# Inner layer norms with features on partitions, and the second half of the merge gate ahead of the key transposes

## What is computed

```python
def layer_norm(x, g, b):
    mu = jnp.mean(xf, axis=-1, keepdims=True)
    var = jnp.mean(jnp.square(xf - mu), axis=-1, keepdims=True)
    y = (xf - mu) * lax.rsqrt(var + LN_EPS) * g + b
...
merged = sigmoid(gate_a + b_gate[0]) * y_a + sigmoid(gate_b + b_gate[1]) * y_b   # token_mixer
return merged @ w_o
...
for l in range(DEPTH):                       # 2 layers
    h = layer_norm(ALPHA * h + mix, ln1_g[l], ln1_b[l])
    f = swiglu(h, ...) if l % 2 == 0 else moe_swiglu(h, ...)
    h = layer_norm(ALPHA * h + f, ln2_g[l], ln2_b[l])
return h[:, N_META:]
```

## Time and profile before

| | |
|---|---|
| median of 3 runs | 2019.66 us (2018.73 to 2020.70) |
| the profiled execution, its own time | 2018.01 us |
| its span, first to last instruction | 2016.3 us |
| TensorE matmul busy | 1914.1 us (95%) |
| VectorE busy | 1400.5 us (69%) |
| ScalarE busy | 1092.7 us (54%) |
| mean granted TensorE clock | 0.963 |
| HBM read | 486.74 MB, 242 GB/s over the span |

### The profile page before, as it was taken

One profiled execution on the slowest core, in us unless ns is written; L12 is line 12 of the kernel. 1 busy time (PEld: TensorE's weight loads), 2 busy tenths in 40 slices (PEclk: granted clock), 3 DMA queues, 4 the chain that ended last, 5 costly groups with the idle time before them and its releaser, 6 DMA issues.

```text
span 2016.3 us, 29184 instructions
## 1 busy us (share of the span) xinstructions
PE 1914.1 (95%) x11315; PEld 1684.1 (84%) x11315; DVE 1400.5 (69%) x1160; ACT 1092.7 (54%) x800; POOL 9.3 (0%) x21
## 2 busy tenths in 40 slices
PE   7899999899989899996999999999999999999995
PEld 6889999799978799996787887878878788787884
DVE  3555465744455456566788888888888788787886
ACT  3534344343434453442676767767767667676773
POOL 0000000000000000000000000000000000000000
PEclk9989999899988899996999999999999999999998
DMA  7535334363647358342798998989989999899992
GB/s 242 174 121 184 131 126 168 105 209 126 203 70 178 105 161 211 126 153 97 285 364 324 358 362 312 367 306 347 366 302 357 327 348 359 297 368 335 325 364 82
DMA packets 219258, 491.20 MB, mean 244 GB/s; under 512 B 7932, under 2 KB 12792, under 8 KB 219176
## 3 DMA queue, kind: packets, MB, share of 16 engines
q1 hardware_dynamic: 216416, 482.44, 69.8%
q0 software_dynamic: 1360, 5.25, 0.8%
q10 hardware_dynamic: 1400, 2.33, 0.5%
HBM read 486.74 MB, written 1.05 MB: 242 GB/s over the span
## 4 chain that ended last, share of the span: by engine, by line
PE 52%; DVE 1%; issue 0%; ACT 0%; DVEq 0%; ACTq 0%
PE ps L568 10%; PE ps L570 10%; PE ps L569 10%; PE ps L839 5%; PE ps L841 5%; PE ps L842 5%; PE ps L829 1%; PE ps L854 1%; PE ps L853 1%; PE ps L873 0%; PE ps L874 0%; PE ps L789 0%; DVE ag_lo L1708 0%; ACT ag_hi L941 0%; PE ps L861 0%
## 5 line engine op out<-in xcount | busy, mean ns | idle before, releaser
L1641 DVE TENSOR_TENSOR w_lo<-raw,w_hi 128x2048 fp32r<-128x2048 f32 x336 | 763.5, 2288 | 146.3 <-ACT w_hi L941 146.2
L941 ACT ACTIVATE w_hi<-raw 128x2048 fp32r<-128x2048 f32 x336 | 639.0, 1918 | 208.7 <-PE ps L570 113.4
L348 DVE TENSOR_TENSOR w_lo<-raw,w_hi 128x2048 fp32r<-128x2048 f32 (+2 forms) x128 | 278.9, 2189 | 209.9 <-ACT w_hi L341 204.4
L568 PE MATMUL ps<-hT_hi,w_lo 128*128 128x272 f32 (+1 forms) x1392 | 406.6, 292 | 10.0 <-DVE w_lo L348 3.2
L570 PE MATMUL ps<-hT_hi,w_hi 128*128 128x272 f32 (+1 forms) x1392 | 403.8, 290 | 0.0
L569 PE MATMUL ps<-hT_lo,w_hi 128*128 128x272 f32 (+1 forms) x1392 | 403.7, 290 | 0.0
L568 PE MATMUL ps<-w_hi,xg_lo 128*128 128x512 f32 x896 | 360.3, 402 | 2.4 <-issue 2.4
L569 PE MATMUL ps<-w_lo,xg_hi 128*128 128x512 f32 x896 | 354.8, 396 | 0.0
L570 PE MATMUL ps<-w_hi,xg_hi 128*128 128x512 f32 x896 | 354.7, 396 | 0.0
L341 ACT ACTIVATE w_hi<-raw 128x2048 fp32r<-128x2048 f32 (+2 forms) x128 | 233.7, 1832 | 191.8 <-PE ps L570 153.6
L568 PEld LDWEIGHTS ps<-hT_hi,w_lo 128*128 128x128 f32 x1392 | 267.5, 192 | 13.2 <-issue 8.0
(11 more groups left out here) (231 smaller groups left out, 1959.4 us busy)
## 6 DMA issues: line engine op xcount, KB each, us to landing
raw<-in_moe_w_gate SPq DMA_DIRECT2D x112, 1024.0 KB, 6.6
raw<-in_moe_w_up SPq DMA_DIRECT2D x112, 1024.0 KB, 6.4
raw<-in_moe_w_down SPq DMA_DIRECT2D x112, 1024.0 KB, 5.9
raw<-in_w_in SPq DMA_DIRECT2D x64, 1024.0 KB, 8.5
raw<-in_ffn_w_gate SPq DMA_DIRECT2D x10, 1024.0 KB, 5.3
raw<-in_ffn_w_up SPq DMA_DIRECT2D x10, 1024.0 KB, 5.1
raw<-in_ffn_w_down SPq DMA_DIRECT2D x10, 1024.0 KB, 5.2
raw<-in_w_pa SPq DMA_DIRECT2D x8, 1024.0 KB, 5.1
```

The lines of the kernel that those rows point to most:

```text
L348: nc.vector.tensor_tensor(w_lo[:, u % HALVES, 0:k * n], raw[:, u % RAW, 0:k * n], w_hi[:, u % HALVES, 0:k * n].bitcast(F32), ALU.subtract) ...
L568: nc.tensor.matmul(dst, l_lo, r_hi, start=start, stop=False)
L941: return nc.scalar.activation(dst, src, ACT.Copy, **kw)
L1641: tt(w_lo[:, at % HALVES, :], raw[:, at % RAW, :], w_hi[:, at % HALVES, :].bitcast(F32), ALU.subtract).then_inc(lo_ready, 1)
```

## The change

1. The residual of the inner norms is kept transposed and in float32 (`hF`, features on partitions). The start puts x through PSUM into hF and from there into hT_hi. h_tok exists for the experts alone.
2. An inner norm (`feature_norm`, `norm_sums`) adds the product to ALPHA * hF straight from PSUM, squares on ScalarE (`squares`), adds feature tiles elementwise and lets TensorE sum over partitions with a matrix of 1/1024, which gives mean and mean square in every partition. The last unit of wo1 and fd1 is computed bank by bank. Variance, reciprocal and root are passes over 272 (256) columns. Centring, scaling, gain and bias and the hi/lo split go by groups of feature tiles (1, 1, 2, 2, 2), and the first matmuls of the next product wait by group.
3. The two units of weights that come next are split inside the norm (`next_weights`).
4. In layer 1 the router reads hF, a new set x_tok transposes hF back to tokens, ScalarE makes x_hi and ALPHA * h_tok from it, VectorE x_lo.
5. The set gta1 moves from behind gr1 to ahead of g_kt, on every engine and in the stream of weights.
6. POOL's queue loads broadcast rows only for the last norm.

```diff
@@ trunk, buffers and stream @@
+        hF = sb(ctx, "hF", [P, KT, T])
+        acc = sb(ctx, "acc", [P, 4, T])
-        h_tok = sb(ctx, "h_tok", [P, 3, D])
...
             add_cols(w_in, COL["gate_a"])
+            add_cols(w_in, COL["gate_a"] + COLS)
             pair(w_in, COL["gr"])
-            add_cols(w_in, COL["gate_a"] + COLS)
...
-                local("gvt1"); local("g_kt"); local("g_sc")
+                local("gvt1"); weights("gta1", 2); local("g_kt"); local("g_sc")
...
-                weights("wo0", 2); weights("wo1", 2); local("wot0"); local("wot1")
-                local("h1t0"); local("h1t1")
+                weights("wo0", 2); weights("wo1", 2); local("wo_ln")
...
-                    local("route"); local("rank")
+                    local("route"); local("x_tok"); local("rank")
...
+        NORM_GROUPS = [(0, 1), (1, 2), (2, 4), (4, 6), (6, 8)]
+        def norm_tmp(norm, a, b):
+            if norm == 1:
+                return (gT_s, aT_f)[a // 4][:, a % 4:a % 4 + b - a, width(0)]
+            return sgA[:, a:b, width(norm // 2)]
@@ tensor: feature_major, by_bank and normed @@
+                    if by_bank and k0 + kn == depth:
+                        for m in range(4):
+                            for k in range(kn):
+                                last = step(k, m)
+                            if m < 3:
+                                last.then_inc(bank_full, 1)
+                    else:
+                        for k in range(kn):
+                            if normed is not None:
+                                pe.wait_ge(norm_lo_ready, NG * normed + norm_group(k0 + k) + 1)
+                            for m in range(n // P):
+                                last = step(k, m)
@@ tensor @@
+            def norm_sums(l, name, norm):
+                pt = begin(l, name)
+                cols, mean = width(l), table("mean")
+                pe.wait_ge(sums_ready, 2 * norm + 1)
+                nc.tensor.matmul(pt[:, 0, cols], mean, acc[:, 0, cols], start=True, stop=False)
+                pe.wait_ge(summed, 5 * norm + 4)
+                nc.tensor.matmul(pt[:, 0, cols], mean, hF[:, 6, cols], start=False, stop=False)
+                pe.wait_ge(summed, 5 * norm + 5)
+                nc.tensor.matmul(pt[:, 0, cols], mean, hF[:, 7, cols], start=False, stop=True).then_inc(mean_full, 1)
...
@@ tensor, main order @@
                 back(l, (("gvt1", "gv1"),), (srT[:, 4:8, :],), 3)
+                feature_major(l, "gta1", hT_hi, hT_lo, cols)
                 key_tokens(l, "g_kt", None, k_tail)
...
-                feature_major(l, "gta1", hT_hi, hT_lo, cols)
                 pe.wait_ge(o_ready, 2 * l + 1)
...
-                feature_major(l, "wo1", m_hi, m_lo, cols, inside=(4, lambda: back(l, (("wot0", "wo0"),), (sgA[:, 0:4, :],), tiles)))
-                back(l, (("wot1", "wo1"),), (sgA[:, 4:8, :],), tiles)
-                transposes(l, ("h1t0", "h1t1"), h_tok, tiles, norm=2 * l)
+                feature_major(l, "wo1", m_hi, m_lo, cols, by_bank=True)
+                norm_sums(l, "wo_ln", 2 * l)
@@ scalar @@
-                    copy(dst[:, 4 * i:4 * i + 4, width(l)], pt[:, :, width(l)]).then_inc(act_done, 1)
+                    copy(hF[:, 4 * i:4 * i + 4, :], pt[:, :, 0:T]).then_inc(act_done, 1)
+                    act.wait_ge(act_done, r + 1)
+                    copy(dst[:, 4 * i:4 * i + 4, :], hF[:, 4 * i:4 * i + 4, :]).then_inc(x_split, 1)
...
+            def squares(l, names, norm, ahead):
+                r, _ = take(l, names[0])
+                act.wait_ge(summed, 5 * norm + 1)
+                nc.scalar.activation(norm_tmp(norm, 0, 4), hF[:, 0:4, cols], ACT.Square).then_inc(squared, 1)
+                signed_off(r)
+                ahead()
+                nc.scalar.activation(idle_sqrt[:, :], idle_sqrt[:, :], ACT.Sqrt)
+                for m in range(4):
+                    act.wait_ge(summed, 5 * norm + 2 + m)
+                    nc.scalar.activation(norm_tmp(norm, 4 + m, 5 + m), hF[:, 4 + m:5 + m, cols], ACT.Square).then_inc(squared, 1)
+                signed_off(number[l, names[1]])
+            def feature_norm(l, name, norm):
+                act.wait_ge(mean_full, norm + 1)
+                nc.scalar.activation(acc[:, 0, cols], bank(number[l, name])[:, 0, cols], ACT.Square).then_inc(mean_squared, 1)
+                act.wait_ge(inverse_ready, norm + 1)
+                nc.scalar.activation(acc[:, 1, cols], acc[:, 1, cols], ACT.Sqrt).then_inc(deviation_ready, 1)
+                for i, (a, b) in enumerate(NORM_GROUPS):
+                    act.wait_ge(scaled_ready, NG * norm + i + 1)
+                    for k in range(a, b):
+                        y = norm_tmp(norm, k, k + 1)[:, 0, :]
+                        if l == 0:
+                            nc.scalar.activation(hT_hi[:, k, cols], y, ACT.Identity, scale=ln_col(norm, 0, k), bias=ln_col(norm, 1, k))
+                        ins = nc.scalar.activation(hF[:, k, cols], y, ACT.Identity, scale=ln_col(norm, 0, k), bias=ln_col(norm, 1, k))
+                    ins.then_inc(norm_ready, 1)
...
+            _, pt = take(1, "x_tok")
+            copy(x_hi[:, :, :].rearrange("p t (b n) -> p (t b) n", b=2), pt[:, :, :]).then_inc(x_hi_ready, 1)
+            copy(h_tok[:, :, :].rearrange("p t (b n) -> p (t b) n", b=2), pt[:, :, :], scale=float(ALPHA)).then_inc(act_done, 1)
@@ vector: feature_norm @@
+                r = number[l, names[1]]
+                pt = bank(r)
+                split.upto(ends[r])
+                for m in range(4):
+                    if m < 3:
+                        dve.wait_ge(bank_full, 3 * norm + m + 1)
+                    else:
+                        full(dve, r)
+                    h = hF[:, 4 + m, cols]
+                    stt(h, h, float(ALPHA), pt[:, m, cols], ALU.mult, add).then_inc(summed, 1)
+                    if m == ahead_at:
+                        ahead()
+                    if m == 1:
+                        dve.wait_ge(summed, 5 * norm + 3)
+                        settle()
+                        step(tt(acc[:, 0, cols], acc[:, 0, cols], hF[:, 4, cols], add))
+                        dve.wait_ge(squared, 5 * norm + 2)
+                        step(tt(acc[:, 1, cols], acc[:, 1, cols], norm_tmp(norm, 4, 5)[:, 0, :], add))
+                        settle()
+                        tt(acc[:, 0, cols], acc[:, 0, cols], hF[:, 5, cols], add).then_inc(sums_ready, 1)
+                dve.wait_ge(squared, 5 * norm + 3)
+                dve.wait_ge(sums_ready, 2 * norm + 1)
+                tt(acc[:, 1, cols], acc[:, 1, cols], norm_tmp(norm, 5, 6)[:, 0, :], add).then_inc(sums_ready, 1)
...
+                if ahead_at is None:
+                    ahead()
...
+                dve.wait_ge(mean_squared, norm + 1)
+                step(stt(acc[:, 1, cols], pt[:, 1, cols], float(LN_EPS), acc[:, 0, cols], add, ALU.subtract))
+                settle()
+                nc.vector.reciprocal(acc[:, 1, cols], acc[:, 1, cols]).then_inc(inverse_ready, 1)
...
+                centre(0)
+                centre(1)
+                dve.wait_ge(deviation_ready, norm + 1)
+                scale(0)
+                scale(1)
+                centre(2)
+                scale(2)
+                low(0)
+                low(1)
+                centre(3)
+                scale(3)
+                low(2)
+                centre(4)
+                scale(4)
+                signed_off(r)
+                low(3)
+                low(4)
...
+                feature_norm(l, ("wo0", "wo1"), "wo_ln", 2 * l, lambda: next_weights("wo1"), 0)
+                    feature_norm(l, ("fd0", "fd1"), "fd_ln", 1, lambda: next_weights("fd1"), None)
+            dve.wait_ge(act_done, number[1, "x_tok"] + 1)
```

More of the change, by code:

```diff
@@ L83, in host_constants @@
         ident=np.eye(P), cos=np.cos(ang), sin=sign * np.sin(ang), xi=xi, xi_squared=xi ** 2, zeta=zeta, mask=mask,
-        restart=np.broadcast_to(restart, (P, T)), before=(p[:, None] < p[None, :]), ones=np.ones((P, P)),
+        restart=np.broadcast_to(restart, (P, T)), before=(p[:, None] < p[None, :]), ones=np.ones((P, P)), mean=np.full((P, P), 1.0 / D),
         iota=np.broadcast_to(np.arange(2 * P), (P, 2 * P)),
@@ L222, in trunk @@
         plan = sb(moe, "plan", [1, 4], I32)
+        h_tok = sb(moe, "h_tok", [P, 2, D])
+        rows = sb(moe, "rows", [P, 2, D])
         moe.close()
@@ L596, in next_unit, with feature_major @@
                 return unit(w_hi, s, k, n), unit(w_lo, s, k, n), k, n
-            def feature_major(l, name, x_hi_, x_lo_, cols, depth=KT, made_by=None, inside=None, bank_free=None):
+            def feature_major(l, name, x_hi_, x_lo_, cols, depth=KT, made_by=None, normed=None, bank_free=None, by_bank=False):
                 if bank_free:
@@ L720, in _ @@
             pe.wait_ge(x_landed, 48)
-            transposes(0, ("ht0", "ht1"), h_tok, 3)
+            transposes(0, ("ht0", "ht1"), x_tok, 3)
             for l in range(DEPTH):
@@ L1804, in _ @@
```

(5 more changed lines are left out.)

282 lines of the change are left out of this document (127 added, 155 removed).

## The result

The changed kernel took **2006.05 us**, the median of 5 runs (1998.03 to 2007.0); the kernel before, on the same chip, 2018.88 us, the median of 5. The ratio of the runs is 0.9926, interval 0.9914 to 0.9938; that is 14.9 us less, where the two medians differ by 12.8. It is faster, the forecast of 2000.7 us is 5.4 us too low, and the range of 1991 to 2009 holds it.

What follows compares the result with a forecast made beforehand. TensorE, busy 95% of the span, bounds the kernel; gate move -7.9, norms -5.6, -5.2, -1.4, start +1.15 sum to -18.95 us from 2018.01, 1999.1; with 1.65 for the median, 2000.7 us, range 1991 to 2009.

Steps and rivals of the forecast that it cites:

- T0: Last matmul of the product ahead of a norm (w_o, ffn_w_down); first gate matmul forecast 12.5 us after it.
- the price of 0.75 us for a sum: Float32 mean matmul in the norms: 0.56 or 0.98 us at two clock levels, 0.75 taken.
- the far end of 2.2: Norms' reciprocal over 272 columns: 1.75 us taken, 2.2 kept as the upper end of its range.
- In the other norms it cost 7 us of VectorE beside matmuls that did not wait: nothing: Removing gain and bias on token rows in norms other than layer 1's w_o norm saves no time.
- the forecast's own signs of being wrong: Chain from T0 above 16 us, low clock after a norm beyond 5.3 us, or experts over 2 us different.
- its 1.15 us: Start: an extra ScalarE copy for each half of x delays the first matmul 1.15 us, or 0 if hidden.
- The forecast's own ends: Spreads for reciprocal, mean matmuls, slow clock after restarts and start; together 1990 to 2008 us.
- The scores follow dense work; I take them at half their present: Gate move: scores fall from 3.64 and 3.72 us to 1.9 and 2.0 us.
- rival 3: Gate move: key wait becomes a w_lo wait and the lower clock comes anyway; 2005.6 us, chance 0.10.
- 1 (all passes cheap): Norms: 272-element passes all alike, reciprocal included, and mean matmuls at full clock; 1994.5 us, chance 0.12.
- 2: ScalarE's functions ping-pong: Square outside Sqrt's table adds table loads in each norm, 7.7 us; 2008.4 us, chance 0.12.
- 4: Slower: hand-overs between engines over some 20 dependent norm steps; 2024.7 us at 0.4 us more each, chance 0.04.

Runs made afterwards that it cites:

- recip_twice: The changed kernel with the wide reciprocal issued a second time in each inner norm, into a row that nothing reads; 2013.81 us.
- norms_only: The changed kernel with gta1 put back behind gr1, so norms and start alone; 11.3 us below the kernel before.
- gate_only: The kernel before with only gta1 moved ahead of the key transposes, nothing of the norms; 8.4 us below its kernel before (2019.04).
- before_warm: The kernel before with 14, 14 and 10 unread float32 matmuls in TensorE's long pause of each norm; ratio 0.9986, 2.8 us.
- early_gate: The changed kernel with ScalarE's and VectorE's split of gta1's first weight unit put ahead of their waits for the decays; 1998.62 us.
- lo_early: early_gate plus VectorE's two w_lo of each inner norm parted, one ahead of the last four banks, one behind the last add; 1988.61 us.
- lo_early_warm: lo_early with matmuls that nothing reads added in TensorE's pauses around the norms; 0.9842 of the kernel before, against 0.9845 for lo_early.
- after_again: The changed kernel itself, unaltered, profiled once more; the profiled execution took 2000.57 us, 5.7 less than the first.

## Why the forecast was right, and where it was not

**The norms: right.** First gate matmul after T0, 12.5 us forecast, 12.6 measured; behind ffn_w_down 12.9 and 12.9. recip_twice shows that the reciprocal is on that chain. The 12.6 holds only where the sums behind w_o fall into the lower clock, as in both executions of the change; in norms_only they did not, and it was 10.9. So the price of 0.75 us for a sum, between the two ends, is in part luck. Reciprocal 1.75 forecast, 1.85 measured, so the far end of 2.2 falls. So does the estimate of 2.3 us from the Trainium skill (VectorE: DVE Perf Modes, "First, the fixed hardware budget"). ScalarE's passes with scale and bias from memory took 0.60 us where I had 0.43 from a row with neither; in layer 0 they lay beside VectorE's work. The Trainium skill (ScalarE: Activation LUTs, "What ACT_TABLE_LOAD costs") has a fixed part for each activation and 93 ns for each operand read from memory, which makes an estimate of 0.60 us; the trace agrees, and for this pass the page was the better source. Sums: they start 0.46 us apart at the full clock and 0.91 at the lower, for 0.56 and 0.98 kept as ends, so both ends were a little high; the six behind w_o took 4.7 us for 4.5 counted. Forecast -10.8 for the two stages, measured -11.0.

Two sentences on the norms did not hold. "In the other norms it cost 7 us of VectorE beside matmuls that did not wait: nothing": from gk to gta0 the change is 2.45 us shorter, 0.8 of it idle time, a wait for w_lo of 1.4 us for 2.2; norms_only has this gain too (61.05 us), gate_only hardly (63.20). And the low clock was to last no longer than 5.3 us after a norm: it lasted 3.8 us behind w_o, but 5.6 us behind ffn_w_down (584.62 to 590.2, clock 0.50), where the kernel before had 4.0. That is one of the forecast's own signs of being wrong, passed by 0.3 us.

The start met its 1.15 us with 1.10 in one execution; the second took 1.97, and before_warm, which changes nothing there, 0.9 more than the kernel before. So that agreement is luck. The forecast's own ends reach down to 1990 us, 1 us below the range that is said to hold them.

**The gate move: the idle part right, the clock part wrong.** TensorE's wait for w_lo was 1.95 and 2.69 us (forecast 1.8 and 2.5), the scores' 0.40 and 0.35 (0.3). Idle time fell by 2.0 and 2.1 us. The scores did as forecast ("The scores follow dense work; I take them at half their present"). The step that failed is beside that sentence: the sum took their lower clock as gone, and gta1 as "12 us of matmuls, neither more nor fewer" at its old price, although it had put a wait of 1.8 and 2.5 us in front of it. The windows of the changed kernel from gta1 to the scores, and the scores:

```profile
94.89:110.00 15.11, 15.11 (x108) 14.77 (x108) 8.27 (x5) 3.66 (x6) 0.00 (x0) 0.89 0.66 231
110.40:112.40 2.00, 2.00 (x52) 1.96 (x53) 0.00 (x0) 1.30 (x2) 0.00 (x0) 1.00 0.83 311
```

The scores took 2.0 us. But gta1 took 15.1 us at 0.89, where the same 108 instructions in gate_only took 13.6 us at 1.00:

```profile
93.75:107.35 13.60, 13.60 (x108) 13.25 (x108) 8.26 (x5) 3.71 (x6) 0.00 (x0) 1.00 0.61 225
```

The lower clock moved from the scores to the product put before them. In layer 1 the same: 14.3 us at 0.88 where early_gate takes 12.8 at 1.00. That is the forecast's rival 3, at 2005.6 us: its wait for w_lo was counted in the sum, its "lower clock comes anyway" was given a chance of 0.10. It accounts for 1.5 us of each layer. early_gate, lo_early and lo_early_warm show that this wait was worth more than its length.

**A term that the sum did not have.** It held the clock of every stage outside the edits as it was. In the profiled execution the two retention stages cost 3.5 us more and the stretch up to w_o's end in layer 1 another 1.4: 62.44 us at 0.97 against 62.15 at 1.00 with 8 transposes more:

```profile
859.25:921.40 62.15, 59.85 (x504) 59.17 (x502) 36.85 (x33) 23.44 (x24) 0.00 (x0) 1.00 0.44 152
```

```profile
845.28:907.72 62.44, 60.20 (x496) 59.52 (x494) 42.09 (x38) 29.07 (x28) 0.00 (x0) 0.97 0.43 152
```

after_again shows that part of this is chance of the execution: it lost nothing in layer 0's retention. The other part came again: both executions of the change lose the 1.7 us or more in layer 1's retention and hold time at the lower clock on the way to w_o behind it. The median of the 11 runs, 2005.3, still stands 4.6 us above the forecast.

**The norm in layer 1: 2.5 us short.** 1.4 are the row above. Then the router began 10.9 us after T0 for 10.2, 0.2 of that from ScalarE's pass of 0.60 us, which is on the path here, and x_lo 25.6 for 24.75. The 2.75 us that VectorE waited for ScalarE's second copy were in the forecast ("VectorE waits for both"). The gather began 4.25 us after x_lo's start, for 3.98 before. Its wait of 5.1 us is this late x_lo, since the ranks and the selection matrix stand behind x_lo in VectorE's queue.

**Rivals.** 1 (all passes cheap) falls with the 1.85 us. 2 falls: one table load for each norm, three in all; Square and Identity ran under the table of the root without another, and the first squares of each norm under the table that was there before it. The Trainium skill (ScalarE: Activation LUTs, "Table sets: the hidden batching unit") names copy and identity as in every set and is silent on square; the trace shows it beside Sqrt with no load. 3 is what happened at gta1, as said above. 4 falls: hand-overs of 0.04 us held (the root starts at 367.97, the reciprocal ends at 367.93), or the 12.6 and 12.9 us would not have come out.

**Open.** What decides where a stretch at the lower level falls in an execution. The runs show that pauses bring such time on, that shorter pauses bring less, and that part of what is removed in one place appears in another; no run here predicts the place.

## What to carry to other kernels

Price a moved or removed pause in two parts, TensorE's idle time and the clock of the stretch behind it, and trust only the first: it came within 0.3 us a layer, while the lower clock moved to the product behind the new wait and cost 1.5 us a layer more. Look for the work of another engine that stands between a product's last bank and the chain behind it; parting a pair of 2.29 us splits, one ahead and one behind, gained 10.9 us where the whole change had gained 14.9. lo_early takes 1988.61 us, 0.9845 of before, with three small moves in the queues and no matmul added; the one version below it, lo_early_warm (0.9842), cannot be told from it.

## What the runs showed of the hardware

Two executions of one program differed by 3.3 us in a stage with no idle time, 382 matmuls at a mean granted clock of 0.94 or 1.00. A reciprocal took 1.85 us for 128x272 against 0.44 for the pass of that shape before it. Keeping TensorE busy raised the clock of a norm's stage from 0.83 to 0.93, yet the same cure in the kernel before raised it (0.90 to 0.95 behind w_o of layer 0) for a gain of 0.9 us in that stage; half of what its transposes gained there came back as a wait for VectorE. The product gta1 held time at the lower clock in 11 of 12 cases behind a wait of 1.9 to 2.7 us, and in none of six behind one of 0.4 or 1.1.
